# RWKV triangular inverses of three token blocks side by side, in a two-layer hybrid recurrent decoder step

## The reference

```
h = RMSNorm(x);  c = h @ w_in            # 30 column tiles of 128
ya = RWKV-7 time mixing (6 heads), yb = RetNet retention (4 heads), yc = Mamba-2 (6 heads)
x += [ya, yb, yc] @ w_out
h = RMSNorm(x);  x += SwiGLU(h)  (layer 0)  or top-2-of-8 SwiGLU experts (layer 1)
```

```
sa = S @ (-kk);   S = S * w + sa (x) (kk * a) + v (x) k;   y = S @ r
```

## Time and profile before

| | us |
|---|---|
| median of 3 runs | 1585.63 (1583.15 to 1589.67) |
| the profiled execution: span | 1584.4 |
| PE busy in it | 1417.6 (89%) |
| DVE / ACT / POOL busy | 916.4 / 738.3 / 129.7 |
| mean granted TensorE clock | 0.884 of full speed |

### The profile page before, as it was taken

One profiled execution on the slowest core, in us unless ns is written; L12 is line 12 of the kernel. 1 busy time (PEld: TensorE's weight loads), 2 busy tenths in 40 slices (PEclk: granted clock), 3 DMA queues, 4 the chain that ended last, 5 costly groups with the idle time before them and its releaser, 6 DMA issues.

```text
span 1584.4 us, 26377 instructions
## 1 busy us (share of the span) xinstructions
PE 1417.6 (89%) x10263; PEld 1219.3 (77%) x10263; DVE 916.4 (58%) x1440; ACT 738.3 (47%) x1113; POOL 129.7 (8%) x162
## 2 busy tenths in 40 slices
PE   5897889896999999978887988969999999999996
PEld 4885777765999999968766777768778778778774
DVE  4634443435455455455364434254889888888886
ACT  5532321403443234364222231244777877876775
POOL 1112011110000000001121100000000000000000
PEclk9996886856999999989877767669999999999998
DMA  5321211001644444122121110142788887987982
GB/s 219 107 68 45 70 41 69 2 14 72 227 150 153 139 147 147 67 90 94 51 79 40 41 56 2 69 161 86 256 310 310 294 311 274 327 317 265 350 307 107
DMA packets 62215, 235.06 MB, mean 148 GB/s; under 512 B 7072, under 2 KB 7168, under 8 KB 61344
## 3 DMA queue, kind: packets, MB, share of 16 engines
q1 hardware_dynamic: 59472, 217.61, 39.0%
q0 software_dynamic: 2496, 13.71, 2.3%
q10 hardware_dynamic: 144, 2.28, 0.3%
HBM read 225.48 MB, written 8.09 MB: 147 GB/s over the span
## 4 chain that ended last, share of the span: by engine, by line
PE 54%; issue 32%; DVE 7%; ACT 5%; POOL 2%; DMA 0%; POOLq 0%; ACTq 0%; DVEq 0%
PE bank L509 11%; PE bank L510 10%; PE bank L511 10%; PE bank L503 7%; ACT whi L1220 2%; PE bank L631 1%; PE bank L525 1%; PE bank L649 1%; PE bank L663 1%; PE bank L926 1%; DVE wlo L1665 1%; PE bank L877 1%; PE bank L661 1%; PE bank L832 1%; POOL x L2459 1%
## 5 line engine op out<-in xcount | busy, mean ns | idle before, releaser
L1665 DVE TENSOR_TENSOR wlo<-wraw,whi 128x1024 fp32r<-128x1024 f32 x410 | 504.9, 1237 | 309.4 <-ACT whi L1220 304.1
L1220 ACT ACTIVATE whi<-wraw 128x1024 fp32r<-128x1024 f32 x410 | 432.9, 1060 | 371.0 <-PE bank L511 279.7
L509 PE MATMUL bank<-hh,whi 128*128 128x320 f32 x608 | 219.1, 360 | 33.9 <-DVE hl L1689 14.3
L510 PE MATMUL bank<-hl,whi 128*128 128x320 f32 x608 | 206.6, 340 | 0.0
L511 PE MATMUL bank<-hh,wlo 128*128 128x320 f32 x608 | 205.2, 338 | 0.0
L509 PEld LDWEIGHTS bank<-hh,whi 128*128 128x128 f32 x608 | 132.1, 217 | 49.4 <-issue 31.5
L1135 PE MATMUL bank<-whi,hh 128*128 128x512 f32 (+1 forms) x384 | 147.3, 384 | 3.7 <-DVE wlo L1665 3.2
L1137 PE MATMUL bank<-wlo,hh 128*128 128x512 f32 (+1 forms) x384 | 143.3, 373 | 0.0
L1136 PE MATMUL bank<-whi,hl 128*128 128x512 f32 (+1 forms) x384 | 143.0, 372 | 0.0
L510 PEld LDWEIGHTS bank<-hl,whi 128*128 128x128 f32 x608 | 132.7, 218 | 0.4
L511 PEld LDWEIGHTS bank<-hh,wlo 128*128 128x128 f32 x608 | 131.2, 216 | 0.0
(11 more groups left out here) (388 smaller groups left out, 2375.1 us busy)
## 6 DMA issues: line engine op xcount, KB each, us to landing
wraw<-in_w SPq DMA_DIRECT2D x410, 512.0 KB, 4.9
smb<-in_s_ssm POOLq DMA_DIRECT2D x2, 1536.0 KB, 6.8
out_o_ssm<-smb POOLq DMA_DIRECT2D x2, 1536.0 KB, 5.4
cst<-in_consts ACTq DMA_DIRECT2D x1, 2225.0 KB, 12.7
srw<-in_s_rwkv POOLq DMA_DIRECT2D x2, 768.0 KB, 4.4
out_o_rwkv<-srw POOLq DMA_DIRECT2D x2, 768.0 KB, 3.6
x<-in_x SPq DMA_DIRECT2D x1, 1280.0 KB, 5.6
out_y<-x SPq DMA_DIRECT2D x2, 640.0 KB, 2.9
```

What stands on the lines that cost most here:

```text
L509: mm(out, hi, rh, start=first, stop=False)
L510: mm(out, hi, rl, start=False, stop=False)
L1220: af(whi[:, ring % HI, :], wraw[:, POS[ring], :], ACT.Copy).then_inc(S("slot_hi"), 1)
L1665: tt(wlo[:, POS[ring], :], wraw[:, POS[ring], :], whi[:, ring % HI, :].bitcast(F32), ALU.subtract).then_inc(S("slot_split"), 1)
```

## The change

- The inverses of all three blocks run level by level, blocks in the order 2, 0, 1 inside a level. Each block has one PSUM bank of its own (`INV_BANK`: 3, 4, 2); both half products of a block go into that bank, one behind the other. `A`, `Wm`, `TM` and `TT` have a place per block; the first three and `brx` lie in the part of the weight ring that is free while the layers mix.
- All three A are made first; C and then B are made per block later, just before its chunks, C alone in two steps and B in two more (`reads`), in banks `BC_BANKS`.
- The last level of a block makes TT alone.
- The twelfth projection slot goes ahead of the A products; bonus sums and gate projection go into level 1 of the inverses, in banks 0, 1, 5. `sample_states`, `steps`, the tokens of block 2 and its reads and chunk lie between later levels.
- The 18 later slots are cut into halves of 12 matmuls, with other work between. Retention follows the inverses, Mamba starts behind the last chunks of block 1.

```diff
-RW_AT = [92.0, 148.0, 56.0]
...
+TURNS = [2, 0, 1]
+INV = [(q, b) for q in range(max(LEVELS)) for b in TURNS if q < LEVELS[b]]
...
+INV_BANK = [3, 4, 2]
+A_BANKS = [(4, 5), (0, 1), (2, 3)]
+BC_BANKS = [(3, 4), (3, 4), (2, 5)]
...
+RW_CH = [112.0, 139.0, 94.0]
+CHS = 10.0
...
+def inv_at(q, b):
+
+    return 64.0 + 8.0 * (q - 1) + 0.7 * RW_POS[b]
...
+N_WHOLE = 12
+SPREAD = [60.4, 63.3] + [inv_at(q, 2) + w for q in range(1, 6) for w in (2.6, 6.8)] + [105.8, 107.8, 109.2, 111.2] \
+    + [RW_CH[0] + CHS * c + w for c in range(2) for w in (1.3, 3.6, 5.8, 8.6)] + [133.8, 135.5] \
+    + [RW_CH[1] + CHS * c + w for c in range(2) for w in (1.3, 3.6, 5.8)] + [161.0, 164.0, 171.0, 175.0]
+DN = [7 + 4.2 * j for j in range(N_WHOLE)] + SPREAD[0::2]
...
-MB_AT = [152.0, 200.0, 173.0]
+MB_AT = [161.0, 221.0, 183.0]
```

The levels of an inverse on TensorE:

```diff
+                for q in range(1, LEVELS[b]):
+                    at = inv_at(q, b)
+                    yield at
+                    pe.wait_ge(S("rw_T"), inv(l, q - 1, b))
+                    for h in range(HA):
+                        for r in halves:
+                            m = mm(B[bk][r, h * CH:(h + 1) * CH], A[r, b, h, :], TM[r, b, h, :], start=True, stop=True)
+                    m.then_inc(S("rw_W"), 1)
+                    yield at + 4
+                    pe.wait_ge(S("rw_Wc"), inv_step(l, q, b))
+                    if q < LEVELS[b] - 1:
+                        for h in range(HA):
+                            for r in halves:
+                                mm(B[bk][r, h * 32:(h + 1) * 32], TT[r, b, h, :], half1(Wm[r, b, h, :], q, 0),
+                                   start=True, stop=True)
+                    for h in range(HA):
+                        for r in halves:
+                            m = mm(B[bk][r, (HA + h) * 32:(HA + h + 1) * 32], Wm[r, b, h, :], half1(TT[r, b, h, :], q, 1),
+                                   start=True, stop=True)
+                    m.then_inc(S("rw_TW"), 1)
```

and on VectorE:

```diff
+                for q in range(1, LEVELS[b]):
+                    at = inv_at(q, b)
+                    yield at + 1.5
+                    v.wait_ge(S("rw_W"), inv(l, q, b))
+                    tt(Wm_, b64(bk, HA, rr), rep(lev[rr, q, :], HA), ALU.mult).then_inc(S("rw_Wc"), 1)
+                    yield at + 6
+                    v.wait_ge(S("rw_TW"), inv_step(l, q, b))
...
+                        if odd or q < LEVELS[b] - 1:
...
+                            m = tt(part, part, got, ALU.add)
+                    m.then_inc(S("rw_T"), 1)
```

C and B of a block on TensorE (k from 0 to 3: C for both halves of the heads, then B for both):

```diff
+                    if k >= 2:
+                        pe.wait_ge(S("rw_C"), done + k - 1)
+                    elif k == 0:
+                        pe.wait_ge(S("rw_T"), inv(l, LEVELS[b] - 1, b))
...
+                    lhs, rhs = ((aa, Pi), Dx[:, 3:6, :]) if k < 2 else ((Pi,), X2)
+                    for z, lh in enumerate(lhs):
...
+                    m.then_inc(S("rw_sC"), 1)
```

More of the change, by code:

```diff
@@ L124 @@
 CHUNKS_OF = [2, 2, 1]
-LEV = 6.2
-CHS = 8.0
-RW_AT = [92.0, 148.0, 56.0]
[L128 to L141, removed]
@@ L142 @@
-DN = HALVES[0::2]
-DH = [d + 0.01 for d in DN]
-DE = [h + 3.8 for h in DN]
+TURNS = [2, 0, 1]
+INV = [(q, b) for q in range(max(LEVELS)) for b in TURNS if q < LEVELS[b]]
+INV_STEP = [(q, b) for q, b in INV if q]
+INV_BANK = [3, 4, 2]
+A_BANKS = [(4, 5), (0, 1), (2, 3)]
+BC_BANKS = [(3, 4), (3, 4), (2, 5)]
+TOK_BANKS = [(3, 4, 3), (3, 4, 3), (5, 5, 5)]
+SA_BANK = [3, 3, 2]
+RW_POS = [TURNS.index(b) for b in range(3)]
+AT_A = [58.5, 59.2, 58.0]
+AT_W0 = [61.0 + 0.7 * k for k in RW_POS]
+BC_AT = [104.5, 132.5, 81.8]
@@ L288, in trunk @@
         norm_at = top[0]
[L289 removed]
+        TT = sb("TT", [P, 3, HA, CH])
+        Bm = sb("Bm", [P, 2, TA, CH])
         htmp = sb("htmp", [P, 2, T], offset=norm_at)
@@ L620, in rwkv @@
[L620 to L633, removed]
@@ L942, in parts_of @@
             def parts_of(l):
+                for b in TURNS:
+                    yield inverse(l, b)
                 for b in range(3):
+                    yield reads(l, b)
+                    yield tokens(l, b)
                     yield rwkv(l, b)
-                    yield tokens(l, b)
                 yield sample_states(l)
@@ new lines, in reads @@
+            def reads(l, b):
+                rr, cb, done = slice(0, BLOCKS[b][1]), 5 * l + RW_CHUNKS[b], 12 * l + 4 * RW_POS[b]
+                sfx = "8" if b == 2 else ""
+                for k in range(4):
+                    o, bk = k % 2, BC_BANKS[b][k % 2]
+                    yield BC_AT[b] + (1.0, 1.7, 3.0, 3.7)[k]
+                    if k == 0 and cb:
+                        v.wait_ge(S("rw_y"), cb)
+                    v.wait_ge(S("rw_sC"), done + k + 1)
+                    if k < 2:
+                        tt(C12[rr, o, :, :, :].rearrange("p z t c -> p (z t) c"), b64(bk, 2 * TA, rr),
+                           rep(C("incl" + sfx, rows=rr), 2 * TA), ALU.mult).then_inc(S("rw_C"), 1)
+                    else:
+                        tt(Bm[rr, o, :, :], b64(bk, TA, rr), rep(C("strict" + sfx, rows=rr), TA), ALU.mult)\
+                            .then_inc(S("rw_C"), 1)
```

268 lines of the change are left out of this document (132 added, 136 removed).

## The result

| | before | changed |
|---|---|---|
| median of 4 runs each, us | 1586.84 (1583.15 to 1589.67) | **1505.09** (1502.91 to 1506.44) |
| profiled execution: span | 1584.4 | 1504.6 |
| PE busy in it | 1417.6 | 1348.6 |
| mean granted TensorE clock | 0.884 | 0.922 |

The ratio is 0.9486, with a 95% interval of 0.9469 to 0.9504: 81.7 us faster, where 56 had been forecast (1529).

What follows compares the result with a forecast made beforehand. Idle TensorE and its low clock were taken to bound the two mixing stretches. Per layer, 205 work + 43 idle + 32 excess = 280 us against 306.5, 28 saved with the 1.2 ahead: 1529 us, range 1474 to 1580.

Steps and rivals of the forecast that it cites:

- behind them: Reads, chunks and retention after the inverses: 97 us work, 9 idle and 12 excess per layer.
- Mamba: Three Mamba blocks at each mixing stretch's end: 83 us per layer, 30 of them idle and 16 excess.
- What bounds it: Mixing stretch per layer: 208 us full-clock work, 42 idle, 56 excess from low clock; gains must come from the last two.
- Inverses side by side: Inverse levels: other blocks' products and half slots cover DVE's answers; 72 us at full clock, 4 idle where 30 were.
- Halves: Later projection slots: each half, 1.8 us, covers waits on DVE in levels and chunks; no gain of its own.
- rival 1: Ahead of Mamba, half slots do not lift the clock: 334 us per layer, 1637 in all; chance 0.11.
- Dropped products: Last level of each block's inverse makes TT alone: 3 us less work per layer.
- Slot 12 ahead of A: Before the first products, the slot fills an idle wait behind six matmuls: 1.2 us gained per layer.
- C and B per block: Made later, before the chunks: same matmuls, four DVE waits instead of two, covered; nothing, uncovered about 1 us per wait.
- the rival that it takes 110 us: Mamba's three blocks, delayed by ACT and DVE queues, give the gain back: about 1583 us; chance 0.12.
- The output projection: After layer 0's mixing stretch: it begins 28 us earlier, a sign that the forecast is right.
- Rival 3, the clock held throughout,: Ahead of Mamba the clock never falls, and Mamba takes 75 us: 250 us per layer, 1470 in all; chance 0.20.

Runs made afterwards that it cites:

- experiments 2: The changed kernel with the inverses run block after block (2, 0, 1), halves kept: 1516.24 us, ratio to the kernel before 0.9559.
- experiment 3: The changed kernel with inverses block after block and the 18 later projection slots whole again: 1567.17 us, ratio to the kernel before 0.987.
- experiment 1: The changed kernel with its 18 later projection slots whole again, each at its first half's place: 1540.13 us, ratio to the kernel before 0.971.
- experiment 5: The changed kernel with the last level making TM as well again, read by nobody: 1511.24 us, ratio to the kernel before 0.9516.
- experiment 10: The changed kernel with the twelfth whole slot behind the A products instead of ahead: 1496.77 us, ratio to the kernel before 0.9428.
- experiment 12: The changed kernel with the twelfth slot behind the A products and idle matmuls in Mamba's waits: 1472.54 us, ratio to the kernel before 0.9273.
- experiment 4: The kernel before with its 19 later projection slots in halves: four executions, 1567.8, 1593.8, 1594.4 and 1597.3 us, no ratio given.
- experiment 9: The changed kernel with unread idle matmuls ahead of Mamba's long waits and the output projection: 1480.88 us, ratio to the kernel before 0.9317.

## Why the prediction was right, and where its terms were off

The forecast's own sum, term by term, per layer. Excess is taken at 0.44 of the time at 1.2 GHz, all of it in the first two parts; of Mamba's I take 20 us (layer 0) and 22 (layer 1) to be idle, which is an estimate, so its split into work and excess is one too.

| us per layer | forecast | layer 0 | layer 1 |
|---|---|---|---|
| inverses: work / idle / excess | 72 / 4 / 4 | 65.6 / 3.1 / 3.2 | 65.6 / 3.1 / 3.2 |
| behind them | 97 / 9 / 12 | 100.0 / 5.9 / 9.1 | 100.1 / 5.9 / 9.1 |
| Mamba | 36 / 30 / 16 | 34.2 / 28.4 / 15.1 | 33.3 / 27.6 / 18.2 |
| sum, length | 280 | 264.6 | 266.1 |

- **What bounds it.** "What the change brings must come out of the last two", idle and excess. Right for excess, which went from 56 us to 27 and 30, where 32 had been forecast. Idle went from 42 to 37, forecast 43, and work from 208 to 200, forecast 205. Layer 0 misses the forecast by 15.4 us: 5.6 idle (1.3 of them because my stretch before ended that much behind the last norm), 5.2 work, 4.6 excess. Layer 1 misses it by 13.9: 6.4, 6.0 and 1.5. All three err the same way. That the excess came out near is in part luck: its 4 and 12 us ahead of Mamba were put by judgement, and what keeps it low, the halves, was not what the sum credited.
- **Inverses side by side.** Idle 4, measured 3.1, with the waits on the identities in it: right, and there is no wait on DVE between the products of a level. The work was taken at 72 us and is 66; that is the term that was mis-sized most, added up from single products; that they overlap more than I allowed is likely but was not taken apart. But I gave the credit for the 30 idle us of before to the order of the blocks. One by one there are only 8.6 us, and with whole slots 9.7 (experiments 2 and 3), so side by side took away 6. The rest went by something that those kernels share with the change; likely it is that the levels stand together with the slots and with the bonus, gate and sample block's pieces in one stretch, which no run undid.
- **Halves.** I gave them no term of their own: in the sum they are cover ("half a slot (1.8 us)" ahead of each answer of DVE), and only rival 1 asks what they do to the clock. They are the largest single part, 35 us (experiment 1), 28 of them by the clock, and 51 where the inverses run one by one (3 against 2).
- **Dropped products.** Forecast 3 us per layer, measured 3.2 and 3.9 (experiment 5).
- **Slot 12 ahead of A.** "The slot fills the wait: 1.2 us gained." This step failed: with the slot behind A there is no wait ahead of A either, so it is the bonus sums' and gate projection's going that took the 1.23 us away, and the 2.6 us on the identities, where VectorE's masks have no cover now, are gone too. The move costs some 3 us per layer (experiment 10).
- **C and B per block.** Nothing forecast. What shows is one wait of 0.55 us in the inverses and 0.9 behind them: right, with that.
- **Mamba.** 83 us forecast, 77.7 and 79.1 measured; 30 us idle forecast, 28 measured: right, and the rival that it takes 110 us is out. Its clock is 0.65 and 0.60, where 0.5 to 0.6 had been named.
- **The output projection** of layer 0 was to begin 28 us earlier and begins 41.6 earlier; the difference is the miss above.
- **Rival 1, halves do not lift the clock,** is refuted by its own measure, a clock under about 0.77 ahead of Mamba: it is 0.92, and whole slots are what costs. **Rival 3, the clock held throughout,** came half way, 265 us between 280 and 250; with it held to the end, the part behind would be 106 us for 115.

Of the 81.7 us, 62 go to halves and side by side together (experiment 3) and 6 to the dropped products. The other 13 or 14 are a net: the twelfth slot's place took 8 away, so the order behind the inverses (retention beside the chunks, block 1's levels no longer beside Mamba, C and B later) should have brought some 20. No run took these apart, and differences of 9 us by the clock of one part lie between executions of the same instructions as well.

## What to carry to other kernels

Don't price a new order by the idle time that it covers: here that fell by some 4 us per layer and the time by 40, the clock of the work around the waits being the larger part. What paid in this kernel: wide products cut into halves and spread between the narrow ones (35 us), and products that nobody reads in the long waits that were left (24 us). Ahead of the identities (waits of 2.20, 0.80 and 0.17 us) and of levels where no wait was left, such products cost 17 us on balance. Read two kernels part by part, and each part's clock: equal instructions differed by up to 12 us in a part of 106.

## What the hardware showed that I had not expected

- **A TensorE without a gap loses the clock.** The 7 us at 1.2 GHz in the inverses of the changed kernel lie in one place, in windows of 2 us of layer 0:

```profile
112.00:114.00 2.00, 2.00 (x48) 1.81 (x47) 0.81 (x4) 0.00 (x0) 1.50 (x1) 1.00 0.00 0
114.00:116.00 2.00, 2.00 (x73) 2.00 (x73) 0.66 (x3) 0.00 (x0) 0.71 (x1) 1.00 0.03 8
116.00:118.00 2.00, 2.00 (x54) 2.00 (x52) 0.30 (x2) 0.00 (x0) 0.00 (x0) 0.66 0.00 0
118.00:120.00 2.00, 2.00 (x43) 2.00 (x42) 0.62 (x2) 0.00 (x0) 0.00 (x0) 0.50 0.03 8
120.00:122.00 2.00, 2.00 (x17) 1.96 (x16) 0.00 (x0) 0.55 (x2) 0.00 (x0) 0.50 0.00 0
122.00:124.00 2.00, 2.00 (x12) 1.81 (x10) 0.00 (x0) 0.00 (x0) 0.00 (x0) 0.63 0.00 0
```

PE is never idle in the profile (which models the ends of matmuls, so that busy is not the same as at its peak). From 112.4 to 120.6 us stands the longest run of narrow products without a slot, level 2's second products with the sample states; the clock falls in it at 116 and comes back inside the half slot that follows. In experiment 12 it falls in the same products of layer 1, at 720 us, stays down through the whole half slot (724.9 to 728.4) and comes back at 730 us, amid the first products of level 3, which are narrow. So the width of the products does not decide it alone. The Trainium skill, "TensorE: Matmul & The Clock Gate", Part 1, says that activity lifts the throttle and an idle spell brings it back. That agrees with Mamba, where filling the waits took the clock from 0.65 to 0.85, and not with these rows. What it is in these products that lets the clock fall was not isolated.
- **Equal instructions, other clock.** The part behind the inverses took 106.0, 106.3, 110.6, 115.0 and 118.5 us in executions of the same instructions, in several of these kernels and in both layers, with 5.9 us idle in each, at clocks of 1.00, 1.00, 0.95, 0.91 and 0.88. The Trainium skill, on the same page, Part 1, says that the moment at which the clock rises varies from run to run, and that the ramp costs a typical kernel under 1%. The first agrees. The second speaks of a warm-up; here the clock falls and rises again within the kernel, and that makes 12% of a part. One kernel's executions lie up to 14 us apart (experiment 10), in experiment 4 30.
- **Idle matmuls of ones and identity lift the clock.** These are windows of layer 0's sample block in experiment 9; the group of eleven ahead of its output begins at 300.93. In the changed kernel 300 to 310 us have 0.50 throughout.

```profile
300.00:302.00 2.00, 1.69 (x9) 1.57 (x10) 1.82 (x4) 0.26 (x1) 1.02 (x1) 0.54 0.00 0
302.00:304.00 2.00, 2.00 (x13) 2.00 (x13) 2.00 (x2) 0.00 (x0) 1.72 (x1) 0.61 0.00 0
304.00:306.00 2.00, 2.00 (x45) 1.81 (x43) 0.20 (x1) 0.00 (x0) 0.00 (x0) 1.00 0.00 0
```
